# Three passes of one decoder layer joined into one program, with the first tiles of each stage placed by hand among the steps of the last tile before

## The reference

```python
h = rms_norm(x, norm_w);  p = h @ w_in           # columns: attention q | k | v | gate, HGRN2 q | f | i | gate
q, k = rms_norm(q, q_norm_w), rms_norm(k, k_norm_w)          # per head of 64
a = sink_attention(q, k, v)                      # window 128, the meta tokens always visible, a learned sink per head
f = lb + (1 - lb) * sigmoid(f);  S_t = diag(f_t) S_{t-1} + (1 - f_t) i_t^T;  o_t = S_t^T silu(q_t)
y = x + [a * silu(gate_a) ; rms_norm_head(o) * silu(gate_h)] @ w_out
```

## Time and profile before

| | us |
|---|---|
| median of 3 runs | 1266.8 (1266.02 to 1267.26) |
| profiled execution, its own time | 1269.48 |
| its span, first to last instruction | 1267.7 |
| PE busy | 1196.4 (94 %) |
| DVE / ACT / POOL busy | 630.6 (50 %) / 399.3 (31 %) / 264.6 (21 %) |
| mean granted TensorE clock | 0.964 |

### The profile page before, as it was taken

One profiled execution on the slowest core, in us unless ns is written; L12 is line 12 of the kernel. 1 busy time (PEld: TensorE's weight loads), 2 busy tenths in 40 slices (PEclk: granted clock), 3 DMA queues, 4 the chain that ended last, 5 costly groups with the idle time before them and its releaser, 6 DMA issues. The chain is left out here.

```text
span 1267.7 us, 25817 instructions
## 1 busy us (share of the span) xinstructions
PE 1196.4 (94%) x9462; PEld 979.7 (77%) x9462; DVE 630.6 (50%) x1688; ACT 399.3 (31%) x1178; POOL 264.6 (21%) x274
## 2 busy tenths in 40 slices
PE   6999999999999999984699999999999985999998
PEld 5777777777777777764578888888888864888887
DVE  6655555555555555553365555555565544222221
ACT  7311222222222222111235555555555553101010
POOL 0003222222222222223022232232232210000000
PEclk9989999999999999996699999999999977999999
DMA  7532111111111111100812111111112005343341
GB/s 266 168 116 78 60 59 58 58 58 58 58 58 58 54 56 45 39 17 28 286 69 77 42 64 60 41 55 69 41 45 79 10 9 199 134 149 109 139 149 67
DMA packets 48033, 104.10 MB, mean 82 GB/s; under 512 B 5664, under 2 KB 18592, under 8 KB 47968
## 3 DMA queue, kind: packets, MB, share of 16 engines
q1 hardware_dynamic: 47856, 103.42, 23.0%
q10 hardware_dynamic: 128, 0.03, 0.0%
HBM read 66.17 MB, written 38.26 MB: 82 GB/s over the span
## 5 line engine op out<-in xcount | busy, mean ns | idle before, releaser
L309 POOL TENSOR_TENSOR h_lv<-h_lv,h_tt 128x256 f32<-128x256 f32 x96 | 85.0, 885 | 282.9 <-PE h_near_a L796 97.1
L530 DVE TENSOR_TENSOR h_lv<-h_lv,h_tt 128x256 f32<-128x256 f32 x96 | 40.9, 426 | 154.8 <-PE h_near_a L796 70.6
L1922 PE MATMUL o_bank_y<-o_w_hi,o_m_hi 128*128 128x512 f32 x272 | 109.9, 404 | 3.7 <-DVE o_w_lo L1870 2.1
L770 PE MATMUL h_bank_b<-h_w_hi,h_h_hi 128*128 128x512 f32 x256 | 107.7, 421 | 0.1
L1924 PE MATMUL o_bank_y<-o_w_hi,o_m_lo 128*128 128x512 f32 x272 | 107.2, 394 | 0.0
L770 PE MATMUL h_bank_a<-h_w_hi,h_h_hi 128*128 128x512 f32 x256 | 107.1, 418 | 0.0
L1923 PE MATMUL o_bank_y<-o_w_lo,o_m_hi 128*128 128x512 f32 x272 | 106.9, 393 | 0.0
L771 PE MATMUL h_bank_b<-h_w_lo,h_h_hi 128*128 128x512 f32 x256 | 101.7, 397 | 0.0
L772 PE MATMUL h_bank_b<-h_w_hi,h_h_lo 128*128 128x512 f32 x256 | 101.5, 396 | 0.0
L771 PE MATMUL h_bank_a<-h_w_lo,h_h_hi 128*128 128x512 f32 x256 | 101.3, 396 | 0.0
L772 PE MATMUL h_bank_a<-h_w_hi,h_h_lo 128*128 128x512 f32 x256 | 101.3, 396 | 0.0
(11 more groups left out here) (284 smaller groups left out, 2796.0 us busy)
## 6 DMA issues: line engine op xcount, KB each, us to landing
h_split<-h_h_hi SPq DMA_DIRECT2D x17, 512.0 KB, 3.4
h_split<-h_h_lo SPq DMA_DIRECT2D x17, 512.0 KB, 4.1
a_h_hi<-h_split SPq DMA_DIRECT2D x17, 512.0 KB, 3.5
a_h_lo<-h_split SPq DMA_DIRECT2D x17, 512.0 KB, 4.3
h_x<-x_prompt SPq DMA_DIRECT2D x16, 512.0 KB, 3.5
o_m<-mixed SPq DMA_DIRECT2D x16, 512.0 KB, 5.0
o_x<-x_prompt SPq DMA_DIRECT2D x16, 512.0 KB, 4.3
y_prompt<-o_y SPq DMA_DIRECT2D x16, 512.0 KB
```

The source lines that it names most:

```text
L309: ins = pool.tensor_tensor(new[:, :, 0, :], old[:, :, 0, :], right.unsqueeze(2).to_broadcast([P, HW // (2 * b), b]), ALU.mult)
L770: pe.matmul(out[:, :], h_hi[t.slot][:, k, :], hi, start=(k == 0), stop=False)
L1922: pe.matmul(out, hi, w_hi[:, k, cols(a)], start=(k == 0), stop=False)
```

## The change

The three passes become one program. Each is now a stage whose steps for each engine are generators, and `output_pass` calls them in a hand-written order, one order for each engine. So the first tiles of the attention stage are placed among the steps of the last HGRN2 tile, and the first output tile among the steps of the last attention tile. SBUF is given out by hand: attention weights are loaded into the places of HGRN2 weights as soon as the last projections that read them are done, four rows of blocks in one DMA, and the output weights (four DMAs) into places free after the samples' attention; their split stands at the ends of the last six peeled attention tiles. Output tiles are now 16 prompt tiles, and the sample rows are the last tile. The output stage has one PSUM bank for turned tiles instead of two, attention one `mix` buffer instead of two, and the reciprocal of the gate is done in place.

```diff
@@ attention stage: sync, gpsimd, scalar, tensor @@
+            sp.wait_ge(before["f_proj"], TILES)
+            load_weights(0)
+            sp.wait_ge(before["q_proj"], TILES)
+            load_weights(1)
+            sp.wait_ge(before["i_proj"], TILES)
+            load_h(tile(0, 0))
+            load_h(tile(0, 1))
+            load_weights(2)
+            sp.wait_ge(before["g_proj"], TILES)
...
+            sp.wait_ge(g_proj, TILES)
+            yield
+            store_mixed(tile(0, TILES - 2))
+            store_mixed(tile(0, TILES - 1))
 
             sp.dma_start(new_win_k, k_nat[:, :]).then_inc(rest_stored, 16)
             sp.dma_start(new_win_v, v_nat[:, :]).then_inc(rest_stored, 16)
+            sp.wait_ge(mix_stored, 16 * TILES)
+            yield
...
             pool.wait_ge(sink_loaded, 5 * 16)
             k_rstd_of(tile(0, 0))
+            yield
             k_rstd_of(tile(0, 1))
+            yield
+            pool.wait_ge(before["g_proj"], TILES)
+            pool.memset(VMD[:, :], 0.0)
+            pool.memset(KTS[:, :, :, :].bitcast(F32), 0.0)
...
             q_rstd_of(tile(0, 0))
             q_weight(tile(0, 0))
+            yield
...
             split_weights(0)
-            split_weights(1)
+            yield
             keys_values(tile(0, 0))
+            yield
...
             act.dma_start(new_meta_v, v_nat[0:META, :]).then_inc(meta_stored, 16)
+            split_weights(1)
             keys_values(tile(0, 1))
+            yield
+            square_q(tile(0, 0))
+            split_weights(2)
+            square_q(tile(0, 1))
+            yield
+            gate(tile(0, 0))
...
             project(t0, kv_bank(t0), 0, range(KT), True).then_inc(kv_proj, 1)
+            yield
             pe.wait_ge(h_loaded[1], 32)
+            pe.wait_ge(before["g_silu"], TILES)
             project(t1, kv_bank(t1), 0, range(KT)).then_inc(kv_proj, 1)
+            yield
...
+            pe.wait_ge(q_normed, 1)
+            project(t0, kv_bank(t0), 2, range(KT), True).then_inc(g_proj, 1)
+            yield
@@ output stage: tensor @@
+            t0, t1 = tile(0, 0), tile(0, 1)
+            pe.wait_ge(attention["q_placed"], 2 * (TILES - 1))
+            turn(t0, 0)
+            yield
+            turn(t0, 1)
+            yield
+            pe.wait_ge(w_ready, W_DONE + 2 * KT)
+            multiply(t0, 0, range(0, 4))
+            yield
+            multiply(t0, 0, range(4, KT)).then_inc(multiplied, 1)
+            yield
+            multiply(t0, 1, range(0, 4))
+            yield
+            turn(t1, 0)
+            multiply(t0, 1, range(4, KT)).then_inc(multiplied, 1)
+            yield
+            turn(t1, 1)
+            pe.wait_ge(attention["m_ready"], 4 * (TILES - 1))
+            iteration(t1, tile(0, 2))
@@ output_pass @@
+    with nc.Block() as block:
...
+        @block.tensor
+        def _(pe):
+            h, a, o = hgrn.tensor(pe), attention.tensor(pe), output.tensor(pe)
+            next(h)
+            next(a)
+            next(h)
+            next(a)
...
+            pe.wait_ge(attention.sems["k_placed"], 2)
+            next(h)
+            next(a)
+            next(o)
+            next(a)
+            next(o)
+            next(o)
+            next(a)
```

More of the change, by code:

```diff
@@ L320, in _, with iteration @@
             o_rstd(0)
-            def iteration(t0, t2, tail=True, more=True, last=False):
+            def iteration(t0, t2, tail=True, more=True):
                 k_levels(t0, 0, 1)
@@ L708, in iteration @@
                 near_mask(t0, 0)
-                if not ahead:
-                    q_levels(t0, 4, 5)
                 if tail:
@@ L740, in _ @@
                     iteration(*iteration_args(it, c))
-            for n in range(LAST + 1, TILES):
-                iteration(*iteration_args(0, n), ahead=n + 1 < TILES, more=n + 2 < TILES)
-            last = tile(0, TILES - 1)
+            for n in range(LAST + 1, TILES - 1):
+                iteration(*iteration_args(0, n), more=n + 2 < TILES)
+            yield
+            last, before = tile(0, TILES - 1), tile(0, TILES - 2)
+            block_totals(last)
+            q_levels(last, 0, 1)
+            g_mul(last)
+            q_levels(last, 1, 2)
+            yield
+            q_levels(last, 2, 3)
+            yield
+            state_step(before)
+            o_var(before.n)
+            near_mask(last, 0)
+            q_levels(last, 3, 4)
+            yield
+            wait(dve, mix_stored, 16 * before.n)
+            mix(before.n, G[before.slot], MIX[before.slot], P)
+            q_levels(last, 4, 5)
+            yield
+            q_levels(last, 5, 6)
+            near_mask(last, 1)
+            near_sum(last)
+            yield
+            q_levels(last, 6, 7)
+            yield
+            q_levels(last, 7, 8)
+            far_copy(last)
+            yield
             o_var(last.n)
@@ L956, in _ @@
                     iteration(tile(it, c), tile(it, c + 1), tile(it, c + 2), tile(it, c - 1))
-            for n in range(LAST + 1, TILES):
-                iteration(tile(0, n), tile(0, n + 1), tile(0, n + 2), tile(0, n - 1), ahead=n + 1 < TILES, more=n + 2 < TILES)
-            last = tile(0, TILES - 1)
+            for n in range(LAST + 1, TILES - 1):
+                iteration(tile(0, n), tile(0, n + 1), tile(0, n + 2), tile(0, n - 1), more=n + 2 < TILES)
+            yield
+            last, before = tile(0, TILES - 1), tile(0, TILES - 2)
+            level(last, 0)
+            level(last, 1)
+            yield
+            outputs(before)
+            pe.wait_ge(q0_done, last.n + 1)
+            turn_k(before)
+            level(last, 2)
+            yield
+            state_product(before)
+            level(last, 3)
+            yield
+            level(last, 4)
+            yield
+            level(last, 5)
+            yield
+            level(last, 6)
+            yield
+            level(last, 7)
+            yield
             outputs(last)
@@ L1704, in iteration @@
                 scores(t0, 0)
-                if not ahead:
-                    for j in range(4):
-                        if j < 3:
-                            scores(t0, j + 1)
-                        if j:
-                            values(t0, j - 1)
-                        turn_p(t0, j)
-                    return
                 pe.wait_ge(g_copied, t0.n + 1)
@@ L1818, in _ @@
+            load_weights(0)
+            load_weights(1)
+            yield
+            for n in range(2):
+                load_mixed(tile(0, n))
+                load_x(tile(0, n))
+            yield
+            with sp.Fori(0, ROWS // 2 - 1) as it:
                 for c in range(2):
```

821 lines of the change are left out of this document (509 added, 312 removed).

## The result

The changed kernel took 1240.56 us (median of 4 runs, 1239.61 to 1241.68) against 1267.03 for the kernel before beside it: a ratio of 0.9787 with an interval of 0.9775 to 0.98, or 26.5 us less. The profiled execution took 1239.61, with a span of 1237.8. The forecast was 1253, that is 13.5 less. The gain is about twice that: the time lies outside the forecast's own range (1246 to 1260) and inside the wider one (1231 to 1265).

The account below looks back on a forecast made before the run. Pass boundaries were taken as the removable bound: PE waits and a low clock in two seams. 9.7 + 4.5 − 0.7 = 13.5 us less than the median 1266.8 gave 1253; own range 1246 to 1260, wider range 1231 to 1265.

Parts of the forecast that it names:

- seam 1: Last HGRN2 projection to first steady attention tile (565.5 to 663.2); forecast to end at 653.5, gain 9.7, bounds 3 and 17.5.
- the first rival: Clock kept and load hidden: PE never waits long enough to lose the clock, third tile lands in time; 1233, chance 0.25.
- the issues on ACT: Seam 1: six DMA issues on ACT, 4.2 us, stand ahead of the first high half for q of tile 0.
- the memsets on POOL: Seam 1: six memsets, 3.5 us, stand ahead of q's factor, on the path to the gate of tile 0.
- the outputs, the turn and level 2: Seam 1, PE steps after the k|v matmuls of tile 1: 5.0 us, ending at 582.6.
- the samples: End of seam 1: turned copies 1.9, scores 2.15, softmax some 3.7, values 5.5; taken at 17 in all.
- Seam 2: Last attention tile to second half of the output pass's first prompt tile (1021.7 to 1080.2); gain 4.5, bounds 2 and 17.
- some 8: Seam 2: PE's wait in us for the third output tile's load, held on SP behind all attention tiles' stores.
- Small terms: Constants' DMAs, output weights' split, tail store and single buffers outside the seams: −0.7 in the sum; steady tiles keep their length.
- The split of the output weights: Six portions at the end of attention tiles, in front of the next tile's steps: −0.8, bounds 0 and −3.
- The slower case: Loads in the way: 9.05 MB through one queue delays ACT's issues and q's weights; 1276, chance 0.11.
- the row on DVE's splits: Seam 1: eight low halves took 6.40 instead of 5.46 beside POOL work; by the port-sharing rule 2 us more, time 1255.

## Why the prediction was right, and where not

- *Where the time lies.* Right for the larger part: the two seams gave 18.9 of the 29.9 us between the profiles. But of the 16.4 us by which this gain exceeds the forecast, 11.7 lie outside the seams (7.5 ahead of seam 1, 2.8 in the attention tiles, 1.4 at the end), where the prediction looked for next to nothing. That the time still fell between 1231 and 1265 is partly luck: it is nearer to the first rival's 1233 than to 1253, without that rival's condition.
- *Seam 1, a gain of 9.7.* It was 10.2, and both steps named as its limits, the issues on ACT and the memsets on POOL, were confirmed by moving them (4.4 and 2.6). Of the single steps two errors cancelled. The recurrence was put to end 71 us behind the last HGRN2 projection and ended 66.9 behind it, mainly because q started 2.2 sooner (the outputs, the turn and level 2 took 2.8 at the full clock and not 5.0). And the samples took 20.6 instead of 17: 3.7 until their scores and not 1.9, and the values 9.9, at the lower clock throughout.
- *Seam 2, a gain of 4.5.* Right in mechanism, the wait of "some 8" us being 7.97, but mis-sized: 8.7 was measured. The recorded terms themselves give 4.2 (1076 to 1080.2), and the pieces listed up to 1034.5 add up to 1032.9. The rest is three steps. The last tile ended 1.9 earlier in the stretch than worked out. From there to the turn it took 8.4 and not 9.3, as the load took 3.85 and not 5.0. The turn and the 24 products behind it took 7.7 and not 9.5: in the output pass before, the products alone took 7.4 (1059.13 to 1066.55), and 9.5 is reached only with the 2.10 us of waiting for the weights' split ahead of them, which the change removes.
- *Small terms, −0.7.* This is the step that failed. "One mix buffer, one bank for turns and the reciprocal in place ... nothing": the placing of SBUF by hand, of which these are part, was taken for a matter of room, and its effect on PE's pace was asked nowhere. In the HGRN2 stage it is worth some 5 us. The split of the output weights, costed at 0.8 lost, didn't show: the attention stretch became 2.0 shorter. Why is open. 512-column matmuls follow one another every 228 ns there and not every 233, 256-column ones every 119 and not every 115; with the attention buffers padded in the kernel before they came every 232 and 119, so the place of `h` does not explain the faster ones.
- *The rivals.* The clock was not kept. The loads were in time for PE; DVE stood 4.4 us for the masks, off the path. The slower case had nothing for it. The 2 us that the row on DVE's splits allowed for did not come either: the two splits took 5.39 and 5.76 us, and POOL worked beside the second for 0.6 us only.

## What to carry to other kernels

Ask of an interleaved seam what each queue holds behind a wait: here a load that needed nothing new stood behind a wait for all stores, and cost as much as the whole seam gained. Memsets on POOL can hold DVE up as well, so they belong where no result of either engine is awaited. When buffers move, compare the pace of steady loops before and after; the place of a stationary operand showed only there.

## What the runs showed of the hardware

- With f32r operands of 128 x 128 as stationary and 512 columns moving, an HGRN2 tile of 96 such matmuls took 31.64 to 31.78 us in the profiles with the stationary buffers at a multiple of 128 bytes, and 32.04 to 32.11 with them 32 or 64 bytes beyond, at the full granted clock: about 3.7 ns a matmul (an estimate, if it is spread over all of them). In the attention stage the same move made no tile shorter.
- Beside memsets on POOL a DVE instruction of 0.17 us took 2.79, and one of 0.29 took 2.80; with the memsets moved away they took 0.34 and 0.31.
- An earlier start can be paid back in clock: in one profile 1.1 us was gained ahead of a step whose first matmuls then took 0.77 instead of 0.46. No run shows it more than once.
